# A recurrence beside an in-projection: ScalarE's functions made by kind for four tiles, with a buffer for each tile

## The reference

```python
proj = h @ w_in[l]                      # 512 x 2560: xr, xg, q, k, v of 512 columns each
xc = causal_conv(xr, width 4) + conv_b
r = sigmoid(blockwise(xc, w_a) + b_a)
i = sigmoid(blockwise(xc, w_x) + b_x)
log_a = -8 * r * softplus(-lam)
a = exp(log_a)
u = sqrt(-expm1(2 * log_a)) * (i * xc)
h = scan(h_t = a_t * h_(t-1) + u_t)     # over the 512 tokens
y_rnn = gelu(xg) * h
```

## Time and profile before

| | us |
|---|---|
| median of 3 runs | 2645.71 (2645.20 to 2645.98) |
| profiled execution, whole | 2646.76 |
| its span (first to last instruction) | 2644.9 |
| its mean granted TensorE clock | 0.935 |
| PE / DVE / ACT / POOL busy | 2354.4 / 1146.2 / 864.8 / 89.6 |

### The profile page before, as it was taken

One profiled execution on the slowest core, in us unless ns is written; L12 is line 12 of the kernel. 1 busy time (PEld: TensorE's weight loads), 2 busy tenths in 40 slices (PEclk: granted clock), 3 DMA queues, 4 the chain that ended last, 5 costly groups with the idle time before them and its releaser, 6 DMA issues.

```text
span 2644.9 us, 33686 instructions
## 1 busy us (share of the span) xinstructions
PE 2354.4 (89%) x11969; PEld 1640.0 (62%) x11970; DVE 1146.2 (43%) x2215; ACT 864.8 (33%) x1591; POOL 89.6 (3%) x94
## 2 busy tenths in 40 slices
PE   4999999999998999999999978789988599988884
PEld 2777567888876775678888746658866233333331
DVE  3435755534535347655345354463143232333334
ACT  2323743322323236533223245452231122222222
POOL 0000000000000000000000000000000211111110
PEclk7998799999999997999999979899998799999997
DMA  8573035323335740133233212203314299999995
GB/s 257 162 189 96 2 128 144 96 88 96 96 73 138 183 126 1 33 106 102 81 103 96 88 40 72 72 11 110 123 49 205 95 398 391 389 409 402 397 401 218
DMA packets 274348, 414.41 MB, mean 157 GB/s; under 512 B 21578, under 2 KB 249458, under 8 KB 261746
## 3 DMA queue, kind: packets, MB, share of 16 engines
q1 hardware_dynamic: 258177, 398.25, 44.0%
q0 software_dynamic: 11840, 8.47, 1.0%
q10 hardware_dynamic: 4144, 5.15, 0.6%
HBM read 420.17 MB, written 25.19 MB: 168 GB/s over the span
## 4 chain that ended last, share of the span: by engine, by line
PE 76%; DMA 8%; DVE 7%; ACT 4%; issue 4%; SPq 0%; POOL 0%; ACTq 0%; DVEq 0%; PEldq 0%; POOLq 0%; PEld 0%
PE bank L675 9%; PE bank L676 9%; PE bank L677 9%; DMA arena<-in_expert_up_w 6%; PE bank L628 6%; PE bank L629 6%; PE bank L630 6%; PE bank L1051 5%; PE bank L1060 3%; PE bank L1052 3%; PE bank L722 2%; PE bank L608 2%; PE bank L696 2%; PE bank L712 2%; PE bank L655 1%
## 5 line engine op out<-in xcount | busy, mean ns | idle before, releaser
L628 PE MATMUL bank<-hT_r,arena_r 128*128 128x512 f32 x704 | 298.7, 424 | 62.3 <-DVE arena_r L1557 28.2
L1051 PE MATMUL bank<-arena,xT 128*64 128x512 f32 x560 | 268.3, 637 | 48.6 <-DMA arena<-in_expert_up_w 26.2
L630 PE MATMUL bank<-hT_r,arena_r 128*128 128x512 f32 x704 | 280.1, 398 | 0.0
L677 PE MATMUL bank<-hT_r,arena_r 128*128 128x512 f32 x704 | 275.4, 391 | 0.0
L1052 PE MATMUL bank<-arena,xT 128*64 128x512 f32 x560 | 268.9, 638 | 0.0
L629 PE MATMUL bank<-arena_r 128*128 128x512 f32 x656 | 261.9, 399 | 0.0
L676 PE MATMUL bank<-arena_r,S_r 128*128 128x512 f32 x528 | 207.0, 392 | 0.0
L628 PEld LDWEIGHTS bank<-hT_r,arena_r 128*128 128x128 f32 x704 | 136.0, 193 | 106.5 <-issue 34.8
L2032 DVE TENSOR_TENSOR S<-S,bank 64x512 f32<-64x512 f32 x80 | 54.8, 685 | 333.3 <-ACT S L1507 259.4
L1051 PEld LDWEIGHTS bank<-arena,xT 128*64 128x64 f32 x560 | 79.8, 146 | 170.6 <-issue 165.9
L630 PEld LDWEIGHTS bank<-hT_r,arena_r 128*128 128x128 f32 x704 | 135.8, 193 | 29.8
(11 more groups left out here) (383 smaller groups left out, 4301.4 us busy)
## 6 DMA issues: line engine op xcount, KB each, us to landing
arena<-in_expert_gate_w SPq DMA_DIRECT2D x32, 2048.0 KB, 14.0
arena<-in_expert_up_w SPq DMA_DIRECT2D x32, 2048.0 KB, 18.8
arena<-in_expert_down_w SPq DMA_DIRECT2D x32, 2048.0 KB, 19.5
arena<-in_w_up SPq DMA_DIRECT2D x88, 512.0 KB, 5.0
arena<-in_w_in SPq DMA_DIRECT2D x68, 512.0 KB, 6.9
arena<-in_w_down SPq DMA_DIRECT2D x40, 512.0 KB, 4.1
arena<-in_w_mod SPq DMA_DIRECT2D x16, 1024.0 KB, 9.9
S<-in_w_mod SPq DMA_DIRECT2D x32, 512.0 KB, 4.7
```

Source lines behind the costliest of these rows:

```text
L628: mm(b[:, :], w_h, hT_r[:, k, :], start=start, stop=False)
L630: return mm(b[:, :], w_l, hT_r[:, k, :], start=False, stop=stop)
L677: return mm(b[:, :], w_slot(arena_r, i, piece)[:, at:at + P], hi, start=False, stop=stop)
L1051: mm(bank[half][gate0:gate0 + SUB, :], x, expert_weights(slot, 0)[:, k, :], start=k == 0, stop=k == KD - 1)
```

## The change

Three things are changed; the products on PE and the loads stay as they are.

1. Every c gets buffers of its own. `r_gate` lies in four tiles of `tmp` and later takes Tanh, 2t/(1+t) and Sqrt in place; `i_gate` takes the tiles of `xr`, which the convolution has read; `a_rec` takes the half of `v` that the attention's output fills later; Gelu is made in place in xg; `h_rec` alternates between two.
2. ACT makes each function for all c together: Sigmoids stay behind evictions 8 to 11, all Exp and the first Tanh stand behind eviction 12, the other Tanh behind 13 and its split, Gelu behind 14 and 15, Sqrt behind 17 and 18.
3. DVE has the branch in three pieces (`rec_gated`, `rec_root`, `rec_scan`), with `proj_rest2` of slots 8 to 11 between them by hand.

```diff
-        r_gate, i_gate, a_rec, u_tmp = hn[:, 0, :], hn[:, 1, :], rot[:, 0, :], rot[:, 1, :]
-        h_rec, g_rec = gpad[:, 0, 0:T], gpad[:, 1, 0:T]
+        r_gate = [hn[:, 0, :], hn[:, 1, :], rot[:, 0, :], rot[:, 1, :]]
+        i_gate = [S[:, c, :] for c in range(CT)]
+        h_rec = [gpad[:, 0, 0:T], gpad[:, 1, 0:T]]
...
+        a_rec, g_rec = o2, qk[:, 4:8, :]
...
                 if 8 <= h < 12:
                     c = h - 8
-                    if c >= 1:
-                        act.wait_ge(s["rec_ready"], c)
-                    for m, g in enumerate((r_gate, i_gate)):
+                    for m, g in enumerate((r_gate[c], i_gate[c])):
                         act.wait_ge(s["gate_done"], 2 * c + m + 1)
                         at = (E_BA, E_BX)[m] + c
                         af(g, bank[2 + 2 * (c % 2) + m][:, :], ACT.Sigmoid, bias=pc2[:, at:at + 1]).then_inc(s["gates_ready"], 1)
-                    act.wait_ge(s["gates_ready"], 2 * c + 1)
-
-                    af(a_rec, r_gate, ACT.Exp, scale=pc2[:, NPRM2 + c:NPRM2 + c + 1]).then_inc(s["rec_act"], 1)
-                    af(u_tmp, r_gate, ACT.Tanh, scale=pc2[:, NPRM2 + 4 + c:NPRM2 + 5 + c]).then_inc(s["rec_act"], 1)
+                if h == 12:
+                    act.wait_ge(s["gates_ready"], 2 * CT)
+                    for c in range(CT):
+                        af(a_rec[:, c, :], r_gate[c], ACT.Exp, scale=pc2[:, NPRM2 + c:NPRM2 + c + 1]).then_inc(s["rec_a"], 1)
+                for c in {12: (0,), 13: (1, 2, 3)}.get(h, ()):
+                    af(r_gate[c], r_gate[c], ACT.Tanh, scale=pc2[:, NPRM2 + 4 + c:NPRM2 + 5 + c]).then_inc(s["rec_t"], 1)
+                for c in {14: (0, 1), 15: (2, 3)}.get(h, ()):
+                    af(g_rec[:, c, :], g_rec[:, c, :], ACT.Gelu_apprx_tanh).then_inc(s["rec_g"], 1)
+                for c in {17: (0, 1), 18: (2, 3)}.get(h, ()):
                     act.wait_ge(s["rec_u"], c + 1)
-                    af(u_tmp, h_rec, ACT.Sqrt).then_inc(s["rec_act"], 1)
-                    af(g_rec, qk[:, 4 + c, :], ACT.Gelu_apprx_tanh).then_inc(s["rec_act"], 1)
+                    af(r_gate[c], r_gate[c], ACT.Sqrt).then_inc(s["rec_s"], 1)
...
+            def rec_gated(c):
+                dve.wait_ge(s["gates_ready"], 2 * c + 2)
+                vec.tensor_tensor(xc[:, c, :], xc[:, c, :], i_gate[c], ALU.mult).then_inc(s["rec_in"], 1)
+            def rec_root(c):
+                dve.wait_ge(s["rec_t"], c + 1)
+                link(vec.tensor_scalar(h_rec[c % 2], r_gate[c], 1.0, None, ALU.add))
+                link(vec.reciprocal(h_rec[c % 2], h_rec[c % 2]))
+                stt(r_gate[c], h_rec[c % 2], 2.0, r_gate[c], ALU.mult, ALU.mult).then_inc(s["rec_u"], 1)
+            def rec_scan(c):
+                dve.wait_ge(s["rec_s"], c + 1)
+                dve.wait_ge(s["rec_in"], c + 1)
+                link(vec.tensor_tensor(xc[:, c, :], xc[:, c, :], r_gate[c], ALU.mult))
+                dve.wait_ge(s["rec_a"], c + 1)
+                link(vec.tensor_tensor_scan(h_rec[c % 2], a_rec[:, c, :], xc[:, c, :], 0.0, ALU.mult, ALU.add))
+                dve.wait_ge(s["rec_g"], c + 1)
+                vec.tensor_tensor(xc[:, c, :], h_rec[c % 2], g_rec[:, c, :], ALU.mult).then_inc(s["rec_ready"], 1)
             for c in range(CT):
                 if c % 2:
                     proj_rest2(6 + c // 2)
...
-            for i in range(8, IN2 + 2):
-                proj_rest2(i)
+                rec_gated(c)
+            rec_root(0)
+            proj_rest2(8)
+            rec_root(1)
+            rec_root(2)
+            proj_rest2(9)
+            rec_root(3)
+            for c in range(CT):
+                rec_scan(c)
+                if c % 2:
+                    proj_rest2(10 + c // 2)
```

More of the change, by code:

```diff
@@ L258, in build @@
             hi_ready lo_ready h_lo_ready o_low sub_hi sub_lo fz_hi fz_lo g_ready gated_hi gated_lo_ready gpad_ready conv_done silu_done act_ready toep_in0 toep_in1 toep_in2 toep_in3 mem_in mem_sq mem_std mem_scaled
-            mem_turned mem_ready conv2_ready gate_in gate_done gates_ready rec_act rec_u rec_ready router_in
+            mem_turned mem_ready conv2_ready gate_in gate_done gates_ready rec_in rec_a rec_t rec_u rec_s rec_g rec_ready router_in
             h_tok_turned h_tok_ready h_tok_out x_tok_turned x_tok_ready logits_done group_shifted second_shifted
```

## The result

The changed kernel takes 2627.01 us (median of 6, 2622.53 to 2627.94) against 2645.85 (median of 6): 18.8 us less, ratio 0.9926 with a 95% interval of 0.9913 to 0.9939. That is 0.7% less and clear of the noise, inside the stated range (2619 to 2629) and 3.1 us above the forecast time of 2623.9. The profiled execution took 2622.53 us, the fastest of the six.

A forecast was written before the change was run, and what follows sets the result against it. PE was taken as held by what stands ahead of evictions in ACT's queue: 25.9 us recovered, less 4.1 at the tail, gives 21.8 off 2645.71, so 2623.9 us, range 2619.0 to 2629.0.

The forecast's parts named there:

- Loss of 25.9 us on PE: In-projection of the second block: PE loses 19.3 us waiting for evictions and 6.4 at lower clock, all to be recovered.
- ACT's batches hidden: In-projection: ACT's functions grouped by kind fit within the tile time of 5.45 us, so they cost nothing.
- DVE's order hidden: In-projection: DVE's roots ahead of weight-split rests 8 and 9 delay no tile, with margins of 4 and 4.4 us.
- rival B: DVE becomes the bound within the projection, PE waits for split weights; 16.3 us saved, 2629.4 us; chance 12%.
- The tail gives back 4.1 us: Between last eviction and attention: late Sqrt and DVE's scans delay the first score reduction, leaving 21.8 of 25.9 us.
- Rival A: Nothing given back before the attention, scans hidden or paid for by better clock; 25.9 us saved, 2619.8 us; chance 6%.
- One load costs 1.28 us: Ahead of the first Sqrt: one ACT table load takes 1.28 us, without the skill's extra drain of 1.38.
- rival E: A table switch costs ACT twice the load ahead of the first Sqrt; 20.5 us saved, 2625.2 us; chance 4%.
- Rival D: In-projection: evictions between the kinds of function bring back six table loads; 21 us saved, 2624.7 us; chance 3%.
- Rival C: PE's clock stays low in the attention, 26.5 us more there; kernel slower at 2650.4 us; chance 2%.
- unknown: the clock: Start of the attention: a low-clock phase of PE may be missed or come twice; taken as nothing, 2.5 us either way.

## Why the prediction was right, and where it was off

- **Loss of 25.9 us on PE, all of it gone: right.** Eviction 19 comes 1680.53 - 1612.49 = 68.04 us after eviction 8, forecast 1679.27 - 1611.20 = 68.07. PE waits for no eviction, and its clock is 1.00 throughout.
- **ACT's batches hidden: right, and tighter than it sounds.** The batch at eviction 12 ended 0.35 us before eviction 13 (forecast 1645.35 - 1644.9 = 0.45). Behind it stood the slack of one accumulator.
- **DVE's order hidden, rival B: did not come.** Rests 8 and 9 start 38.27 and 49.44 us after eviction 8 (forecast 1649.5 and 1660.8, or 38.3 and 49.6).
- **The tail gives back 4.1 us: right.** First scan group 60.99 us after eviction 8 (forecast 61.0), first reduction 77.17 (77.3), 9.1 us behind eviction 19. The runs with Sqrt a tile later (+3.87) and a tile earlier (-4.0) show that this chain is the path. Rival A falls with them.
- **One load costs 1.28 us, rival E: did not come.** The load at 1671.52 ends at 1672.80 and Sqrt starts at 1672.81. The page ScalarE: Activation LUTs of the Trainium skill (What ACT_TABLE_LOAD costs) counts a drain of 1.38 us as well; this trace shows none.
- **Rival D fell:** four loads in the in-projection, none between kinds and evictions.
- **Rival C did not come:** the clock was at 0.50 for the attention's first 12 us and back at 0.99 in the 33 us after them (28.1 busy), and PE's clock hardly bounds the first part (0.5 us).
- **Off: the term "unknown: the clock", taken as nothing, with 2.5 us either way.** The step looked for it at the attention's start only. It measured +2.8 us, and it lay behind the attention, in the 270 us to the router, where I had assumed that an earlier start changes nothing. Between the traces the stretch saved 21.9 us and the whole span 19.4; the +2.8 is more than that gap, and 0.6 came back ahead of the experts. The last 0.6, down to the 18.8 of the medians, lies within the spread of the executions. The mechanism was right, and the mis-sized term was this one. That the range held it is in part luck: its 2.5 us were priced for another place, and only happen to be of the size that appeared behind the attention.
- **Open:** two variants have medians lower than their traces let expect. Sqrt a tile earlier took 4.0 us off the stretch and 9.3 off the median; their profiled executions were the slowest of the timed ones, and the rest lies in executions without a trace.

## What to carry to other kernels

Ask of every engine that evicts accumulators what stands between two evictions in its queue: a wait for another engine there costs the tensor engine's time once its buffers are used up, while table loads of 1.28 us each that fit into the turn cost nearly nothing (13 of them instead of 4, with the functions back at their old places: 1.3 us). Give a chain its own buffers so that its links can be moved one tile on, and then follow the last link: here Sqrt one tile earlier and two steps of DVE behind the attention brought 13 us more in the median (9.8 between the traces, 7.8 in the stretch), since the next stage only needed DVE's queue to be free. And when a gain of under 1% comes out 3 us short, read the granted clock of the untouched stages behind, before any other story.

## What the runs showed of the hardware

- Where the tensor engine's clock falls to its low level largely repeats from execution to execution (270.7 us three times; 273.0, 273.0, 273.2 and 274.8), and differs between kernels whose work at that place is the same. The same idle time of 3.2 us was followed by a mean of 0.71 over 5 us in one kernel and of 0.50 in the other. I had expected such stretches to average out.
- Behind 32 extra products of 0.24 us each the clock stayed at 1.00 for 5 us more and was at 0.52 over the next 7 us (0.77 over the 15 us).
- Table loads follow without a gap and are followed without one: 1.28 us each, with the next function starting 1.29 to 1.30 us after the load's start.
